# A two-block transformer kernel: the first layer's latent attention interleaved with the context stream, and post-norm gains applied at evacuation

## The reference, cut to what matters

```python
for l in range(2):
    last = l == 1
    h  = _rms(x,  g_attn_pre[l]) * (1.0 + sc_a)  + sh_a
    hc = _rms(xc, g_attn_pre[l]) * (1.0 + csc_a) + csh_a
    ...                                   # q, k, v of both streams
    y = _merge(o_lat[0], o_lat[1], o_lat[2], lam, lam_init, g_diff_sub[l]) @ w_out[l]
    x = x + gt_a * _rms(y, g_attn_post[l])
    if not last:                          # the context: layer 0 only
        yc = _merge(o_ctx[0], o_ctx[1], o_ctx[2], lam, lam_init, g_diff_sub[l]) @ w_out[l]
        xc = xc + cgt_a * _rms(yc, g_attn_post[l])
    hf = _rms(x, g_ffn_pre[l]) * (1.0 + sc_f) + sh_f
    x = x + gt_f * _rms(_swiglu(hf, w_ffn_gate[l], w_ffn_up[l], w_ffn_down[l]), g_ffn_post[l])
    if not last:
        hfc = _rms(xc, g_ffn_pre[l]) * (1.0 + csc_f) + csh_f
        xc = xc + cgt_f * _rms(_swiglu(hfc, w_ffn_gate[l], w_ffn_up[l], w_ffn_down[l]), g_ffn_post[l])
```

## Time and profile before

| | us |
|---|---|
| median of 3 runs | 2495.97 |
| lowest and highest of the three | 2494.44, 2498.8 |
| the profiled execution, its own time | 2496.97 |
| its span, first to last instruction | 2495.2 |

### The profile page before, as it was taken

The page is one execution under the profiler, slowest core; times in us unless marked ns, Lnnn a source line. Parts: engine busy times, 40 slices in busy tenths (PEclk is TensorE's granted clock), DMA queues, the critical chain, the costliest instruction groups (busy, mean ns, idle before and its releaser), DMA issues.

```text
span 2495.2 us, 38036 instructions
## 1 busy us (share of the span) xinstructions
PE 2213.4 (89%) x14746; PEld 1989.0 (80%) x14746; DVE 1733.8 (69%) x3402; ACT 1155.1 (46%) x1907; POOL 52.6 (2%) x65
## 2 busy tenths in 40 slices
PE   3998799999999999998968789699989988797997
PEld 2987799999987778887857476699879977567997
DVE  5667678889977777778775565677676665664554
ACT  2543444555554444544444345444454445354443
POOL 1000000000000000000000000000000000000000
PEclk9999899999999999989978769899999998898999
DMA  7648546654467777766622100477657843103664
GB/s 275 202 141 277 186 153 197 212 186 149 148 225 260 261 258 240 247 211 219 223 83 96 34 18 18 137 241 245 223 189 251 255 147 122 51 1 102 186 186 119
DMA packets 137971, 435.04 MB, mean 174 GB/s; under 512 B 15360, under 2 KB 38144, under 8 KB 137280
## 3 DMA queue, kind: packets, MB, share of 16 engines
q1 hardware_dynamic: 109424, 396.93, 49.6%
q10 hardware_dynamic: 25776, 23.97, 2.8%
q0 software_dynamic: 2592, 11.70, 1.3%
HBM read 418.91 MB, written 13.63 MB: 173 GB/s over the span
## 4 chain that ended last, share of the span: by engine, by line
PE 56%; DVE 17%; issue 10%; DMA 10%; ACT 5%; POOL 1%; ACTq 0%; POOLq 0%; SPq 0%; DVEq 0%
PE bk L1657 54%; DVE SPL L1089 4%; DMA TMP<-kept 3%; PE bk L1663 3%; DVE R L1089 2%; DMA RAW<-in_win 2%; DVE RAW L1123 2%; ACT SPL L744 1%; DVE R L1098 1%; ACT R L746 1%; DMA HID<-kept 1%; DMA RAW<-in_peer 1%; DMA kept<-TMP 1%; DVE ST L1104 1%; ACT R L744 1%
## 5 line engine op out<-in xcount | busy, mean ns | idle before, releaser
L1089 DVE TENSOR_TENSOR SPL<-RAW,SPL 128x1024 fp32r<-128x1024 f32 (+1 forms) x614 | 744.8, 1218 | 366.6 <-ACT SPL L744 365.3
L744 ACT ACTIVATE SPL<-RAW 128x1024 fp32r<-128x1024 f32 (+1 forms) x614 | 645.3, 1054 | 617.3 <-PE bk L1657 337.0
L1657 PE MATMUL bk<-HH,SPL 128*128 128x256 f32 x3840 | 747.8, 288 | 22.5 <-DVE SPL L1089 14.0
L1657 PEld LDWEIGHTS bk<-HH,SPL 128*128 128x128 f32 x3840 | 620.6, 194 | 28.1 <-ACT SPL L744 12.6
L1657 PE MATMUL bk<-SPL,WHL 128*128 128x512 f32 x2328 | 555.2, 392 | 16.3 <-DVE WHL L1089 10.3
L1657 PE MATMUL bk<-HL,SPL 128*128 128x256 f32 x1920 | 547.0, 285 | 0.0
L1657 PEld LDWEIGHTS bk<-SPL,WHL 128*128 128x128 f32 x2328 | 428.4, 188 | 111.5 <-issue 23.4
L1657 PEld LDWEIGHTS bk<-HL,SPL 128*128 128x128 f32 x1920 | 372.3, 194 | 2.7 <-issue 0.2
L1657 PE MATMUL bk<-SPL,HH 128*128 128x256 f32 (+1 forms) x1664 | 320.8, 295 | 41.1 <-DVE SPL L1089 26.6
L1657 PEld LDWEIGHTS bk<-SPL,HH 128*128 128x128 f32 x1664 | 273.6, 202 | 49.9 <-issue 29.4
L744 ACT ACTIVATE R<-bk 128x512 f32<-128x512 f32 (+5 forms) x376 | 186.1, 508 | 255.6 <-PE bk L1657 225.2
(11 more groups left out here) (126 smaller groups left out, 1957.3 us busy)
## 6 DMA issues: line engine op xcount, KB each, us to landing
RAW<-in_peer SPq DMA_DIRECT2D x256, 512.0 KB, 4.7
RAW<-in_ada SPq DMA_DIRECT2D x144, 512.0 KB, 4.8
RAW<-in_ffn SPq DMA_DIRECT2D x132, 512.0 KB, 4.2
RAW<-in_win SPq DMA_DIRECT2D x96, 512.0 KB, 4.6
RAW<-in_ffd SPq DMA_DIRECT2D x66, 512.0 KB, 4.2
RAW<-in_wout SPq DMA_DIRECT2D x32, 512.0 KB, 4.5
kept<-TMP ACTq DMA_DIRECT2D x88, 128.0 KB, 3.2
TMP<-kept ACTq DMA_DIRECT2D x66, 128.0 KB, 5.6
```

The lines of the kernel that those rows point to most:

```text
L744: ins = e.activation(out, in_, func, bias=bias, scale=scale)
L1089: e.tensor_tensor(out, a, b, op).then_inc(*dve.up(*points))
L1657: ins = e.matmul(out, lhsT, rhs, start=start, stop=stop, skip_group_check=True)
```

## The change

It has four parts.

1. **Order.** In layer 0 the latent's attention is woven with the context's `out_steps`, `pre_steps` and the first 17 of its 22 hidden blocks (with their `ada` steps). The rest of the context's feed-forward is woven with the latent's `out_steps` and `pre_steps`. `sil2` and `sil3` of layer 1 stand at the start of the context's part, and the differential heads' three closing steps come two units earlier in all attentions.
2. **Banks and scratch.** The latent attention of layer 0 takes scores and transposes in banks (5, 6) instead of (0 to 5) and values in 7 instead of (6, 7). The context's gate and up products take bank 4 alone instead of (4, 5). `times_c` gets another scratch area in layer 1, and the differential values take the first bank of `VALUE`.
3. **Post-norm.** The gain is multiplied in by VectorE when a bank is evacuated (`op`, `fo`), ScalarE squares the unscaled result from the same bank with partial sums, `an_a` adds the parts (2 or 4 per row half), and `an_b` is one operation per row half instead of two. A `fy` bank is free after both readers.
4. **Output.** The result is stored in two transfers, each after its own row half.

```diff
@@ attend_steps
-        out += [("df_a", l, s)] * (n == 24) + [("df_b", l, s)] * (n == 27) + [("dT", l, s)] * (n == 30)
+        out += [("df_a", l, s)] * (n == 22) + [("df_b", l, s)] * (n == 25) + [("dT", l, s)] * (n == 28)
@@ make_plan
-    last = [("sil2", 1), ("sil3", 1)] + ada_steps(l1, range(48))
+    last = ada_steps(l1, range(48))
-    plan += weave(chain + qkv_steps(0, 0, True), attend_steps(0, 1)) + attend_steps(0, 0)
-    side = weave(out_steps(0, 1) + pre_steps(0, 1) + ffn_steps(0, 1), last[:26])
-    plan += weave(out_steps(0, 0) + pre_steps(0, 0), side) + [("mods", 1, "a")]
+    plan += weave(chain + qkv_steps(0, 0, True), attend_steps(0, 1))
+    side = [("sil2", 1)] + out_steps(0, 1)[:3] + [("sil3", 1)] + out_steps(0, 1)[3:] + pre_steps(0, 1)
+    side += weave(ffn_steps(0, 1), last[:24])
+    tail = side.index(("fh", 0, 1, NF - 5, 0))
+    plan += weave(attend_steps(0, 0), side[:tail])
+    plan += weave(out_steps(0, 0) + pre_steps(0, 0), side[tail:]) + [("mods", 1, "a")]
@@ SyncE
-            sp.wait_ge(T.at("x3", 1, 0, "f"))
-            e.dma_start(out_d.rearrange("b (i p) d -> p (b i) d", p=P), LX[0]).then_inc(*T.up("d_out", 16, [("stored",)]))
+            for i in range(2):
+                sp.wait_ge(T.at("x3" if i else "x3a", 1, 0, "f"))
+                e.dma_start(out3[:, i, :], LX[0][:, i, :]).then_inc(*T.up(f"d_out{i}", 16, [("stored", i)]))
@@ GpSimd, sil2
-                    pool.wait_ge(T.at("out", ("dT", 0, 0)))
+                    pool.wait_ge(T.at("out", ("dT", 0, 1)), T.at("out", ("tr", 0, 0, "pd", 1)))
@@ ScalarE
             def op(l, s, j):
-                act.wait_ge(T.at("full", key))
-                A(v2(QS[(l, s)]["oY"], 2)[:, :, j * 256:(j + 1) * 256], v2(ps(*key), 2), ACT.Copy, ("out", key))
+                act.wait_ge(T.at("scaled", key))
+                for i in range(2):
+                    A(QS[(l, s)]["junk"][:, 512 * j + 256 * i:512 * j + 256 * i + 256], ps(*key)[:, i * 256:(i + 1) * 256], ACT.Square,
+                      *([("out", key), ("an_s", l, s, "a")] if i else []), accum=stat(40 + 4 * i + j, 1, s))
-            def an_a(l, s, k):
-                squares(v2(q["oY"], 2), stat(8, 2, s), q["junk"][:, 0:1024], ("an_s", l, s, k))
             def fo(l, s):
-                for i in range(2):
-                    key = ("fy", l, s, 2 * i + 1)
-                    A(v2(QS[(l, s)]["oY"], 2)[:, i, 512:1024], ps(*key), ACT.Copy, ("out", key))
+                for c in (2, 3, 0, 1):
+                    key = ("fy", l, s, c)
+                    act.wait_ge(T.at("full", ("fy", l, s)) if c >= 2 else T.at("scaled", key))
+                    A(QS[(l, s)]["junk"][:, 512 * c:512 * c + 512], ps(*key), ACT.Square,
+                      ("squared", key), ("an_s", l, s, "f"), accum=stat(40 + 4 * (c // 2) + c % 2, 1, s))
@@ VectorE
+                room = spare1 if ORDER[n][:2] == ("ada2", 1) else spare[n in in_ext]
+            def op(l, s, j):
+                dve.wait_ge(T.at("full", key), T.at("gB", l, s, "a", 1))
+                tt(v2(QS[(l, s)]["oY"], 2)[:, :, c], v2(ps(*key), 2),
+                   QS[(l, s)]["gB"][:, c].unsqueeze(1).to_broadcast([P, 2, 256]), ALU.mult, ("scaled", key))
             def an_a(l, s, k):
+                rsum(stat(8, 2, s), parts, ALU.add)
             def an_b(l, s, k):
-                    yi = v2(q["oY"], 2)[:, i, :]
-                    stt(yi, yi, r[:, i:i + 1], q["gB"], ALU.mult, ALU.mult)
-                    tt(LX[s][:, i, :], LX[s][:, i, :], yi, ALU.add, ("x3" if i else "x3a", l, s, k))
+                    stt(LX[s][:, i, :], v2(q["oY"], 2)[:, i, :], r[:, i:i + 1], LX[s][:, i, :], ALU.mult, ALU.add,
+                        ("x3" if i else "x3a", l, s, k))
             def fo(l, s):
-                for i in range(2):
-                    cp(v2(QS[(l, s)]["oY"], 2)[:, i, 0:512], ps(*key), ("out", key))
+                for c in range(4):
+                    dve.wait_ge(T.at("full", ("fy", l, s)) if c < 2 else T.at("squared", key), T.at("gB", l, s, "f", 1))
+                    tt(v2(QS[(l, s)]["oY"], 2)[:, c // 2, h], ps(*key), QS[(l, s)]["gB"][:, h], ALU.mult, ("scaled", key))
@@ TensorE
-            SCORE = {(0, 1): (0, 1, 2), (0, 0): (0, 1, 2, 3, 4, 5), (1, 0): (0, 1, 2, 3, 5)}
-            VALUE = {(0, 1): (3, 4), (0, 0): (6, 7), (1, 0): (6, 7)}
+            SCORE = {(0, 1): (0, 1, 2), (0, 0): (5, 6), (1, 0): (0, 1, 2, 3, 5)}
+            VALUE = {(0, 1): (3, 4), (0, 0): (7,), (1, 0): (6, 7)}
-                b = take(key, (4, 5)) if n == 0 else ps(*key)
+                b = take(key, (4,) if s else (4, 5)) if n == 0 else ps(*key)
```

More of the change, by code:

```diff
@@ L312, in make_plan @@
     chain = [("peer_out",), ("norm_a", "fin"), ("norm_b", "fin"), ("norm_a", (0, 0, "a")), ("norm_b", (0, 0, "a"))]
-    plan += weave(chain + qkv_steps(0, 0, True), attend_steps(0, 1)) + attend_steps(0, 0)
-    side = weave(out_steps(0, 1) + pre_steps(0, 1) + ffn_steps(0, 1), last[:26])
-    plan += weave(out_steps(0, 0) + pre_steps(0, 0), side) + [("mods", 1, "a")]
+    plan += weave(chain + qkv_steps(0, 0, True), attend_steps(0, 1))
[4 more added lines that the diff above has]
+    plan += weave(out_steps(0, 0) + pre_steps(0, 0), side[tail:]) + [("mods", 1, "a")]
     kv1 = qkv_steps(1, 1, False)
-    ffn = weave(ffn_steps(0, 0)[:-3], last[26:]) + [("mods", 1, "f")]
+    ffn = weave(ffn_steps(0, 0)[:-3], last[24:]) + [("mods", 1, "f")]
     plan += ffn[:60] + weave(ffn[60:], [("norm_k", (1, 1, "a")), ("norm_b", (1, 1, "a"))] + kv1[:4])
@@ L1122, in times_c @@
                         doubles.append(n)
-                    e.tensor_tensor_reduce(out=raw(n) if last else spare[n in in_ext], in0=raw(n), in1=c, scale=1.0, scalar=0.0,
+                    e.tensor_tensor_reduce(out=raw(n) if last else room, in0=raw(n), in1=c, scale=1.0, scalar=0.0,
                                            op0=ALU.mult, op1=ALU.add, accum_out=total).then_inc(*dve.up(("times" if last else "spare", n)))
@@ L1588, in dT @@
                 tt(H[s][1][:, 2:4, :], v2(ps(*key), 2), H[s][0][:, 2:4, :].bitcast(F32), ALU.subtract, ("out", key))
+            def op(l, s, j):
+                key, c = ("op", l, s, j), slice(j * 256, (j + 1) * 256)
+                dve.wait_ge(T.at("full", key), T.at("gB", l, s, "a", 1))
+                tt(v2(QS[(l, s)]["oY"], 2)[:, :, c], v2(ps(*key), 2),
+                   QS[(l, s)]["gB"][:, c].unsqueeze(1).to_broadcast([P, 2, 256]), ALU.mult, ("scaled", key))
             def an_a(l, s, k):
+                parts = v2(stat(40, 8, s), 2)[:, :, 0:4 if k == "a" else 2]
                 dve.wait_ge(T.at("an_s", l, s, k))
+                rsum(stat(8, 2, s), parts, ALU.add)
+                dve.wait_ge(dve.own)
                 mean_eps(stat(8, 2, s), D, "an", l, s, k)
@@ L1651, in take @@
                 if b in held:
-                    pe.wait_ge(T.at("out", held[b]))
+                    pe.wait_ge(*([T.at("squared", held[b]), T.at("scaled", held[b])] if held[b][0] == "fy" else
+                                 [T.at("out", held[b])]))
                 held[b], T.bank[key] = key, b
@@ L1926, in av @@
                     key = ("avd", l, s)
-                    b = take(key, VALUE[(l, s)]) if g == 0 else ps(*key)
+                    b = take(key, VALUE[(l, s)][:1]) if g == 0 else ps(*key)
                     for i in range(2):
```

17 lines of the change are left out of this document (6 added, 11 removed).

## The result

| | before | after |
|---|---|---|
| median of 4 runs, us | 2496.59 | 2519.2 |
| lowest and highest | 2494.44, 2498.8 | 2515.97, 2522.32 |
| span of the profiled execution | 2495.2 | 2514.2 |
| TensorE, VectorE, ScalarE busy | 2213.4, 1733.8, 1155.1 | 2228.6, 1730.8, 1183.7 |

The ratio of after to before is 1.009, with an interval of 1.0073 to 1.0108: 0.9% slower. Forecast were 2490 (2468 to 2506). The measured time lies above that range, and also above the 2512 that the forecast's own worst case for the stretch (27 us lost) would have given.

A forecast was written before the change was run, and what follows sets the result against it. TensorE was taken as the bound. From 2496.97 us, post-norm took 10.7 and the weave added 5 (57 us lost instead of 52): 2491.3, or 2490.3 against the median, given as 2490, range 2468 to 2506.

The forecast's parts named there:

- the forecast's own worst case for the stretch: Woven stretch: each place in (c) costs 6 us and (b) gains nothing; 79 us lost, 27 more than before.
- (c): Latent value products wait for the one value bank to be emptied: five places, 3.8 us each, 19 us lost.
- Table loads: Woven region: Exp and Silu alternate, 30 more loads of 1.28 us on ScalarE; costed at nothing beyond (d).
- (d): One gate bank: TensorE waits where no down product stands between blocks (0 and 1), 3 us each, 6 us lost.
- the slower rival: Woven blocks' table loads exposed on the critical path, eight of fifteen blocks costing 20 us: 2510 us, chance 0.18.
- (a): Start of the weave: dense projection work runs a few us at half clock, 3.5 us lost.
- (b): Context's projection and norms among attention units 0 to 11: queue waits and one bank wait, 15 us lost.
- (e): Second weave and its end: 2 us at the latent norm, 11.5 us at the context's last norm lost.
- Post-norm: Gain at evacuation and squares from the bank shorten exposed norm chains at four places: 10.7 us won, bounds 7.5 to 13.
- the third one: Weave loses what the shorter post-norm gives, value-bank places at 6 us each: 2496 us, chance 0.17.
- That the weave pays: VectorE and ScalarE empty the value bank early, (c) and (d) cost 5 instead of 25 us: 2470 us, chance 0.27.
- The earlier df steps: Differential heads' closing steps, two units earlier: same instructions in time already spent in (c), costed at nothing.

The follow-up runs named there:

- the kernel without a weave: Kernel before with the new post-norm, split output store and the second layer's conditioning load and Silu moved right behind the latent attention; order and banks unchanged: 2460.4 us.
- the fastest kernel: Post-norm kernel without woven attention, plus latent projections placed by hand, context's last norm spread over latent feed-forward chunks, differential closing steps two units earlier: 2440.69 us.
- value-bank kernel: Kernel after with the step that empties the value bank one unit earlier, ahead of the next pair's value product: 2485.11 us, ratio 0.9962.
- gate-bank kernel: The value-bank kernel with the context's hidden block 1 in bank 3 instead of 4: 2473.52 us, ratio 0.9923.

## Why the prediction was wrong

**(c), one value bank: the step that failed.** The mechanism was right, down to five places, the releaser and what stands in the queue. Its size was not. The five stops sum to 25.8 us where 5 x 3.8 = 19 was taken, and giving them back gained 34.1. For the worst place the forecast had counted 4.9 us of queue; at 1667.95 VectorE's part of it takes the 4.2 us from 1663.71 on, nearly as counted, but ScalarE's high half and table load, which the count left out, stand ahead of it. Two of the five were thought covered by a down product; only one (2.58) is short. And a term was missing: TensorE works slowly for some us behind each stop (0.57 above; 0.64, 0.62 and 0.59 in the 6.8 us behind the other three long ones). 34.1 is beyond the 30 (5 x 6) of the forecast's own bound, though by little.

**Table loads, costed at nothing beyond (d): the second step that failed.** They cost 15.7 us in all. A load starts right behind the previous instruction, as the earlier trace rows showed, but the argument went from ScalarE's sum (9.1 of 13.5 us per block) to cover. At the place looked at above there is none: TensorE's last product for the bank of the Silu ended at about 1661.84 (busy 0.24 us in the window from 1661.60), and the Silu came at 1663.30, behind the load. This was the mechanism of the slower rival, with 13 to 20 us as its price, but it was set beside the forecast as another way to go. Both happened: the two gains add up to 48.4.

The Trainium skill ("ScalarE: Activation LUTs", What ACT_TABLE_LOAD costs) gives about 2.66 us per switch, drain included; the same page (Table sets: the hidden batching unit) advises to group calls by set. No run here groups calls, but leaving the switches out gained 15.7 us, so on the advice the runs agree. On the price they don't: 1.28 us, and the next activation starts 1.30 us behind the load's start (1662.00 and 1663.30). For 28 loads it would be an estimated 74 us of ScalarE's time by the page, 36 by the rows; 15.7 were seen in the total.

**(d), the gate bank.** The two stops are 4.07 and 5.04 us, 9.1 against 6 forecast. A second bank for one block gave back about 10 to 12 in the kernel with the early value step.

**(a), (b) and (e).** Start to first hidden block took 66.2 us. By the forecast's work rates (an estimate: about 44.6 us of it is work) the loss is 21.6, against 3.5 + 15. At the other end the stops are 5.26 and 6.88, 12.1 us, against 11.5 forecast, and an estimated 17.7, by the same rates, against 13.5 with the low clock between them. These terms were a little low. Counted as the forecast counts (395.9 us with 52 lost), the whole stretch loses 94 us instead of 57. Of the 37 more, (a) and (b) have 3, (c) 15, (d) 3, (e) 4, and some 12 are small stops and low clock between, which I didn't foresee. The loads' 15.7 us are spread over all of these and are no further term of this sum. How much of (a), (b), (e) and of the 12 has another cause was not tested.

**Post-norm.** Behind the region 13.3 us were won against 10.7. The waits that answer are 4.79 instead of 9.23 and 9.66 instead of 13.39 (timeline of weight loads, after):

```profile
2073.84 0.50 PEld L1668 LDWEIGHTS bk<-R 128*128 128x128 f32 x2 [4.79 <-ACT R L750]
```
```profile
2307.67 2.42 PEld L1674 LDWEIGHTS bk<-cons,R 128*128 128x128 f32 x12 [9.66 <-DVE R L1096]
```

The end, answering, in VectorE's and SyncE's timelines:

```profile
2508.55 2.48 DVE L1101 SCALAR_TENSOR_TENSOR R<-R,ST 128x1024 f32<-128x1024 f32 x2
```
```profile
2509.87 1.54 SPq L640 DMA_DIRECT2D out<-R  x2
```

Three places were forecast at 4, 3.3 and 3.4 us; they gave 4.4 and 3.7 by the waits, and 4.8 at the end (from the first operation on the last banks to the end of the span it takes 9.9 us instead of 14.7). What was left out is most of the part inside the stretch: 10.8 us in the weave, and 9 without it, clear of the attention's own variation. The forecast counted 3.3 of it, inside (b), where 3.4 are seen; the gain at the last norms it didn't count. So this term was too small by 10, and it hid part of what the weave lost: with the old post-norm the same order takes 2543.87 us.

**The old kernel's stop at 1565.18** was not read for its cause. Moving the Silu is worth 11.5 us by the medians (6.9 in the profiled stretch), and the order of the change had that and still lost. Against an order with that step moved, the weave costs 59 us (2519.2 - 2460.4), although it has the earlier differential steps in its favour.

**The rivals.** The slower rival (2510) and the third one (each place of (c) at 6 us) each had a part of what happened: the loads cost 15.7 us, and a place of (c) cost 34.1 / 5 = 6.8. The forecast treated them as alternatives, and both happened at once. That the weave pays needed (c) and (d) at 5 us. With both mended by an index and a bank it came to 2473.52, ratio 0.9923, but that is the moved Silu and the post-norm; the kernel without a weave is at 2460.4. What was to be covered needed no attention: most of the second stage's loss can be covered by projections that stand there anyway (four of about 5.5 us each).

**The earlier df steps** were costed at nothing and gave about 5 us, by the time of one kernel and by the profiles of two pairs. The stretch starts 9.9 us earlier in the kernel after; 5 of that is this, and 3 to 5 us were also seen in the profiles of the four kernels that leave those steps where they were. Nothing in the forecast accounts for either, and without them the kernel after would have been slower still.

## What to carry to other kernels

When two streams are woven into one in-order list and a resource is cut to one bank, look for each step that empties the bank and ask which step of the *other* stream now stands ahead of it on each engine: the price is that whole queue, and moving the emptying step one place can be worth more than the change (34 us here). Cost a stop on TensorE at more than its length, and never cost an instruction at nothing because its engine idles on average; read whether it idles at that place. And before weaving a long chain of small operations into dense work, try to fill the chain's few known stops by hand with the dense steps that stand nearest.

## What the runs showed of the hardware

- In the woven stage of the kernel after, TensorE ran at a low clock behind each of these stops: in the 6.8 us behind the five value stops the granted clock was 0.64, 0.57, 0.76 (the short one of 2.58 us), 0.62 and 0.59, and behind the two gate stops (4.07 and 5.04 us) 0.75 and 0.57. Eight value loads took 2.85 us behind the stop at 1667.95, where eight took 1.49 in the earlier trace rows.
- In the rows here an activation table load (1.28 us) starts as soon as ScalarE has finished the instruction before it (at 1662.00, where that ended at 1661.99), and the activation follows 1.29 or 1.30 us behind the load's start. Such a load can be free (1545.38, where TensorE had no idle time) or stand in TensorE's way (1662.00), by what waits behind it.
- The low clock of the attention alone (0.78 before) is there in the fastest kernel too (0.81). It isn't spread over the attention: before, the granted clock was 0.50 from 1447.7 to 1490 and 1.00 from 1499.7 to 1548. No kernel here settles what would lift it; with dense products woven through it the clock of the woven feed-forward was 0.96 in the value-bank kernel and 0.98 in the gate-bank kernel (0.90 after), and their totals were still 25 and 13 us above the one without a weave.
